# A two-layer hybrid encoder in fp32: another order of VectorE's work around the attention, and the gating of seven convolution rows on GpSimd

## The reference, cut to what matters

```
proj = h @ w_in                       # q, k, v, z, x/B/C, dt: 1024 -> 3872 columns
q, k = rope(q), rope(k)               # 8 query heads, 2 key heads of 64
attn = window_attention(q, k, v)      # |i-j| <= 128, blocks of 128 queries, a sink logit per head
xbc  = silu(conv5(xbc) + b)           # depthwise, width 5, centred; 12 rows of 128 channels
y    = ssd forward + ssd backward + D * x     # Mamba-2, chunks of 128
ssd  = rms_norm(y * silu(z)) * g
h    = layer_norm(alpha * h + [attn, ssd] @ w_out)
gate, val = h @ w_up                  # 2 x 2816
h    = layer_norm(alpha * h + (silu(conv3(gate)) * val) @ w_down)
```

## Time and profile before

| | before |
|---|---|
| median of 3 runs | 1300.85 us |
| the profiled execution | 1301.02 us, its span 1299.2 us |
| TensorE busy | 1280.8 us (99% of the span) |
| VectorE busy | 798.3 us (61%) |
| ScalarE busy | 611.7 us (47%) |
| GpSimd busy | 125.4 us (10%) |
| TensorE's granted clock | 0.999 of full speed |

### The profile page before, as it was taken

One profiled execution on the slowest core, in us unless ns is written; L12 is line 12 of the kernel. 1 busy time (PEld: TensorE's weight loads), 2 busy tenths in 40 slices (PEclk: granted clock), 3 DMA queues, 4 the chain that ended last, 5 costly groups with the idle time before them and its releaser, 6 DMA issues.

```text
span 1299.2 us, 17967 instructions
## 1 busy us (share of the span) xinstructions
PE 1280.8 (99%) x7456; PEld 1059.1 (82%) x7456; DVE 798.3 (61%) x1071; ACT 611.7 (47%) x913; POOL 125.4 (10%) x125
## 2 busy tenths in 40 slices
PE   9999999999999999999999999999999999999997
PEld 9877778889888888888898677778888888888886
DVE  7888898865444444342378988979654444443425
ACT  6767776436333333311286776653553333332112
POOL 2024611001000000000020344000100000000000
PEclk9999999999999999999999999999999999999999
DMA  5464666523323333323144557663233333323322
GB/s 199 158 145 111 134 146 134 176 76 103 98 98 98 97 97 98 130 97 98 53 136 143 132 115 163 130 179 122 73 113 96 97 95 96 96 95 128 97 96 110
DMA packets 43872, 151.36 MB, mean 116 GB/s; under 512 B 4912, under 2 KB 9424, under 8 KB 42640
## 3 DMA queue, kind: packets, MB, share of 16 engines
q1 hardware_dynamic: 38160, 130.01, 30.3%
q0 software_dynamic: 5632, 20.21, 9.3%
HBM read 141.81 MB, written 6.29 MB: 114 GB/s over the span
## 4 chain that ended last, share of the span: by engine, by line
PE 93%; DVE 5%; ACT 1%; issue 1%; DMA 0%; POOL 0%; SPq 0%; DVEq 0%
PE ps L869 18%; PE ps L870 17%; PE ps L871 17%; PE ps L1027 9%; PE ps L1028 9%; PE ps L1029 9%; PE ps L916 5%; PE ps L1241 2%; DVE cv L1476 2%; PE ps L895 1%; PE ps L1255 1%; PE ps L1019 1%; PE ps L1225 1%; DVE ast L1624 1%; DMA raw<-in_units 0%
## 5 line engine op out<-in xcount | busy, mean ns | idle before, releaser
L869 PE MATMUL ps<-hhi,whi 128*128 128x512 f32 x1040 | 410.4, 395 | 4.4 <-DVE cv L1476 3.0
L870 PE MATMUL ps<-hlo,whi 128*128 128x512 f32 x1040 | 405.1, 389 | 0.0
L871 PE MATMUL ps<-hhi,wlo 128*128 128x512 f32 x1040 | 405.0, 389 | 0.0
L618 ACT ACTIVATE whi<-raw 128x1024 fp32r<-128x1024 f32 x208 | 219.5, 1057 | 216.1 <-DMA raw<-in_units 216.1
L1313 DVE TENSOR_TENSOR wlo<-raw,whi 128x1024 fp32r<-128x1024 f32 x170 | 207.9, 1225 | 149.6 <-ACT whi L618 149.6
L869 PEld LDWEIGHTS ps<-hhi,whi 128*128 128x128 f32 x1040 | 195.1, 188 | 53.3 <-issue 7.9
L871 PEld LDWEIGHTS ps<-hhi,wlo 128*128 128x128 f32 x1040 | 195.2, 188 | 41.2
L870 PEld LDWEIGHTS ps<-hlo,whi 128*128 128x128 f32 x1040 | 195.3, 188 | 39.1
L1027 PE MATMUL ps<-whi,uhi 128*128 128x512 f32 x352 | 137.1, 390 | 0.0
L1029 PE MATMUL ps<-wlo,uhi 128*128 128x512 f32 x352 | 137.0, 389 | 0.0
L1028 PE MATMUL ps<-whi,ulo 128*128 128x512 f32 x352 | 136.9, 389 | 0.0
(11 more groups left out here) (182 smaller groups left out, 1540.8 us busy)
## 6 DMA issues: line engine op xcount, KB each, us to landing
raw<-in_units SPq DMA_DIRECT2D x208, 512.0 KB, 3.6
wlo<-in_units POOLq DMA_DIRECT2D x38, 512.0 KB, 5.5
gb<-in_gb SPq DMA_DIRECT2D x5, 1024.0 KB, 5.7
h_kept<-hb SPq DMA_DIRECT2D x2, 2048.0 KB, 9.0
ha<-h_kept SPq DMA_DIRECT2D x2, 2048.0 KB, 9.7
hb<-in_x SPq DMA_DIRECT2D x4, 512.0 KB, 5.9
v_rep<-v_tm SPq DMA_DIRECT2D x32, 64.0 KB, 2.2
out_y<-hb SPq DMA_DIRECT2D x8, 256.0 KB, 2.0
```

The costliest lines, as they stand in the source:

```text
L618: A(whi[:, m % RING, :], raw[:, m % RING, :], ACT.Copy).then_inc(unit_hi, 1)
L869: mm(out, whi[:, slot, cols], xhi, start=start, stop=False)
L870: mm(out, whi[:, slot, cols], xlo, start=False, stop=False)
L871: return mm(out, wlo[:, slot, cols], xhi, start=False, stop=stop)
```

## The change

The schedule and four engines' code for these entries change; the arithmetic is the same.

1. `A0` goes from 8 to 7: each attention turn is one step earlier. `AV_AT` now puts the values products into projections 11, 13, 15 and 16 (before: 11, 13, 15 and 17): relative to the turns they need, blocks 0 to 2 are one projection later, block 3 as before.
2. In an attention step VectorE's order was: mask and maximum, transpose of the last turn, gating of the last row, weight splitting, the first tap or two, denominator, the other taps. It is now: mask and maximum, three taps, denominator, last tap, transpose of the last turn. The taps are four entries (F, F1, F2, F3).
3. The gating of rows 1 to 7 (`SILU_POOL`) is a multiplication on GpSimd, ahead of XS and AN in its step. ScalarE adds the 1 by a second instruction after the tanh (a Copy with bias 1.0), which waits for the tanh. Rows 0 and 8 to 11 stay with VectorE.
4. Unit 11's low part is made by DMA too (`BY_DMA` from 11), so no attention step has a splitting on VectorE.
5. The first scores wait for 3 rotated rows (k and two of q) and the second for all 5, as needed.

```diff
-BY_DMA = range(12, 31)
+BY_DMA = range(11, 31)
+SILU_POOL = range(1, 8)
-A0 = 8
-AV_AT = {A0 + 2 * t + 3: t for t in range(NBLK)}
+A0 = 7
+AV_AT = {A0 + 4: 0, A0 + 6: 1, A0 + 8: 2, A0 + 9: 3}
@@ mixer_schedule
-        if 1 <= i < 9:
-            steps += [("PT", i - 1), ("SIL2", n - 1 - U_CONV)]
-            if n - 1 - U_CONV >= 4:
-                steps += [("XS", n - 1 - U_CONV)]
+        if n - 1 - U_CONV in SILU_POOL:
+            steps += [("SIL2", n - 1 - U_CONV)]
+        if i == 8:
+            steps += [("PT", 7)]
...
         steps += [("SH" if n >= U_CONV else "S", n + AHEAD)]
+        if 1 <= i <= 8 and n - 1 - U_CONV >= 4:
+            steps += [("XS", n - 1 - U_CONV)]
         steps += [("F", n)]
...
-        if 2 <= i < 8:
-            steps += [("F1", n)]
+        if U_CONV <= n < U_Z:
+            steps += [("F1", n), ("F2", n)]
         if 0 <= i < 8:
             steps += [("AD", i), ("AN", i)]
-        if U_CONV <= n < U_Z and not 2 <= i < 8:
-            steps += [("F1", n)]
         if U_CONV <= n < U_Z:
-            steps += [("F2", n)]
+            steps += [("F3", n)]
+        if i == 1:
+            steps += [("SIL2", n - 1 - U_CONV)]
+        if 1 <= i < 8:
+            steps += [("PT", i - 1)]
@@ gpsimd
+                    elif what == "SIL2" and i in SILU_POOL:
+                        pool.wait_ge(conv_tanh, L * N_CONV + i + 1)
+                        pool.wait_ge(silu_done, L * N_CONV + i)
+                        x = bc[:, i, :] if i < 4 else xsc[:, i % 2, :]
+                        nc.gpsimd.tensor_tensor(x, x, cv[:, i % 2, :], ALU.mult).then_inc(silu_done, 1)
@@ scalar
-                        A(dst, cv[:, i % 2, :], ACT.Tanh, scale=0.5).then_inc(conv_tanh, 1)
+                        if i in SILU_POOL:
+                            A(dst, cv[:, i % 2, :], ACT.Tanh, scale=0.5).then_inc(tanh_raw, 1)
+                            act.wait_ge(tanh_raw, L * len(SILU_POOL) + i - SILU_POOL[0] + 1)
+                            A(dst, dst, ACT.Copy, bias=1.0).then_inc(conv_tanh, 1)
+                        else:
+                            A(dst, cv[:, i % 2, :], ACT.Tanh, scale=0.5).then_inc(conv_tanh, 1)
@@ tensor
-                        if i == 0:
-                            pe.wait_ge(rope_done, L * 5 + 5)
-                        else:
+                        if i < 2:
+                            pe.wait_ge(rope_done, L * 5 + (5 if i else 3))
+                        if i:
                             pe.wait_ge(as_exp, L * 8 + i)
@@ vector
-                    elif what == "SIL2":
+                    elif what == "SIL2" and i not in SILU_POOL:
                         dve.wait_ge(conv_tanh, L * N_CONV + i + 1)
+                        if i - 1 in SILU_POOL:
+                            dve.wait_ge(silu_done, L * N_CONV + i)
```

More of the change, by code:

```diff
@@ L335, in trunk @@
         v_done, tanh_done, zs_done = sem("v_done"), sem("tanh_done"), sem("zs_done")
-        v_spread = sem("v_spread")
+        v_spread, tanh_raw = sem("v_spread"), sem("tanh_raw")
         xd_done, seg_full = sem("xd_done"), sem("seg_full")
@@ L1464, in _ @@
                         split(unit(L, i))
-                    elif what in ("F", "F1", "F2") and U_CONV <= i < U_Z:
+                    elif what in ("F", "F1", "F2", "F3") and U_CONV <= i < U_Z:
                         j = i - U_CONV
@@ L1470, in _ @@
                         src = ps[:, unit_bank(i), :].rearrange("p (b s) -> p b s", b=NSEQ)
[L1471 to L1478, removed]
-                    elif what == "SIL2":
+                        n, tap = {"F": (0, 0), "F1": (1, 1), "F2": (2, 3), "F3": (3, 4)}[what]
+                        s = tap - 2
+                        lo, hi = max(0, -s), SEQ - max(0, s)
+                        if n:
+                            dve.wait_ge(conv_taps, L * 4 * N_CONV + 4 * j + n)
+                        V.scalar_tensor_tensor(out=dst[:, :, lo:hi], in0=src[:, :, lo + s:hi + s],
+                                               scalar=pmc("conv_w", 5 * j + tap, 5 * j + tap + 1),
+                                               in1=dst[:, :, lo:hi], op0=ALU.mult, op1=ALU.add).then_inc(conv_taps, 1)
+                    elif what == "SIL2" and i not in SILU_POOL:
                         dve.wait_ge(conv_tanh, L * N_CONV + i + 1)
+                        if i - 1 in SILU_POOL:
+                            dve.wait_ge(silu_done, L * N_CONV + i)
                         x = bc[:, i, :] if i < 4 else xsc[:, i % 2, :]
```

## The result

| | before | after |
|---|---|---|
| median | 1300.76 us (1300.68 to 1300.94, 4 runs) | 1308.81 us (1306.22 to 1310.91, 4 runs) |
| ratio, 95% interval | | 1.006 (1.0048 to 1.0072) |
| profiled execution, its span | 1301.02, 1299.2 | 1310.91, 1309.1 |
| TensorE, VectorE, ScalarE, GpSimd busy | 1280.8, 798.3, 611.7, 125.4 | 1285.1, 793.9, 619.0, 145.8 |
| TensorE's granted clock | 0.999 | 0.995 |

In e5 and e6 one run of ten took several times as long as the others; it is left out of the ranges given for them, and without it their medians are 0.04 and 0.11 us lower than printed.

The account below looks back on a forecast made before the run. TensorE was taken to wait for VectorE's round (7.42 against 6.73 us) and, at SF 0, a chain off TensorE. Both layers together gain 2.5 or lose 0.3 us: 1298.4 to 1301.2, middle 1299.7; range 1295.2 to 1302.6.

Parts of the forecast that it names:

- The gap at SF 0: TensorE before SF 0, end of the chain: a wait of 2.0 us stays, and behind SF 0 nothing is changed.
- the 14.88 from T 7: Chain from T 7 to SF 0: gating ready 4.75 us after T 7, SF 0 another 10.13 later.
- Block 3 in unit 16: Values block 3 on TensorE: moves its 2.3 us ahead of T 7.
- the small operations held: VectorE's 4-column operations, if held by GpSimd: waits up to T 7 of 3.3 us, SF 0 at 153.55.
- row 0's gating: VectorE, step 8: arrives 0.4 us inside GpSimd's scaling, is held until 77.10, ends at 77.66 instead of 76.15.
- AS 3: Scores on TensorE due at 81.98: wait 1.44 us because mask 2 and its exponentials come late.
- rival (a): Step 8: GpSimd holds nothing up, row 0's gating gets in first or between the scaling's instructions; 1295.4 us, chance 0.24.
- the 3.05 row: Step 17 before the change: VectorE's gating of row 10 took 3.05 us instead of 0.65, held through two GpSimd instructions.
- CB 1: TensorE's product needing `alo` of block 1: waits about 0.2 us, or 0.62 if the small operations are held.
- The small terms: Across engines: Copy 0.63 us, GpSimd's gating 1.3, the values' transpose wait gone, 10.13 from gating 9 to SF 0.
- Rival (c): GpSimd's gating starts up to 0.9 us later, meeting small operations in full: 2.2 us more per layer, 1305.6 us, chance 0.15.
- the held case: Whole kernel if VectorE's 4-column operations are held by GpSimd: 0.2 us lost per layer, 1301.2 us as timed.

Follow-up runs that it names:

- e5: The kernel after with GpSimd's product with D (XS) behind its scaling in attention steps: 1303.72 us, ratio 1.0018; no usable trace.
- e6: The kernel after with the gating of rows 1 to 7 back on VectorE, ahead of the taps, and no Copy on ScalarE: 1301.18 us, ratio 0.9999.
- e10: The kernel before with two further caps of 1.14 us each on VectorE, so SF 0 comes 2.28 us later per layer: 1308.74 us, ratio 1.0062.
- e4: The kernel after with values block 3 back in unit 17: 1300.16 us, ratio 0.9993.
- e7: The kernel after with row 10's XS before heads 2 and 3, attention steps' XS behind the scaling, and values block 3 in unit 17: 1294.74 us, ratio 0.9953.
- e1: The kernel after with XS of row 10 ahead of heads 2 and 3 on GpSimd in step 17: 1301.71 us, ratio 1.0005.
- e11: The same edit as e5 on the kernel after (XS behind the scaling in attention steps), run again: 1303.49 us, ratio 1.0015.
- e8: The kernel after once more, unchanged: 1308.33 us, ratio 1.0061.
- e2: The kernel before with XS of row 10 ahead of heads 2 and 3 on GpSimd in step 17: 1298.50 us, ratio 0.9981.
- e3: The kernel before with one more 1.14 us cap on VectorE ahead of the cap that SF 0 waits for: 1304.69 us.
- e9: The kernel after with rows 1 to 7 gated on VectorE, row 10's XS before heads 2 and 3, and values block 3 in unit 17: 1293.05 us, ratio 0.9939.

## Why the prediction was wrong, step by step

- **The gap at SF 0: right in size, wrong in price.** "So a wait of 2.0 us stays at SF 0" and "behind SF 0 nothing is changed". The wait was 2.08 and 2.10. Priced at its own length it is all in the 14.88 from T 7; but behind it TensorE ran 3.4 us at half clock, 1.6 us more, once per layer. This is the step that failed: the kernel before had 0.71 and 1.48 us there, and I counted 2.0 us as more of the same. e10 shows the price on the kernel before, without any of the change.
- **Block 3 in unit 16: the second step that failed.** I moved its "2.3 us ahead of T 7" and looked no further. In layer 1 it cost 3.71 us of stop and 1.7 of half clock. e4 shows that the place does it. The stop of 1.34 us behind block 3 in the trace of before was a sign that I left unread. What stops TensorE is open (below).
- **Up to SF 0 in layer 0 the sum was right, its parts not.** T 7 was forecast for 138.7 with the small operations held; it came at 139.16, or 138.4 without the 0.74 of the start, and SF 0 at 153.56 on that clock against 153.55. That the two agree so closely is luck: T 7 was 0.25 early, and from there SF 0 took 15.14 us, not 14.88. And of the parts, row 0's gating was held for 0.46 us, not 1.5: it got in between the scaling's two instructions, whose pair took 2.49 instead of 2.04 us, so AS 3 waited 0.26 and not 1.44. Here rival (a) was right, and with it my reading of the 3.05 row, held over such a gap, was too strong: in step 17 it held again (2.90), in step 8 not. Against that CB 1 waited 2.11 instead of 0.62 us.
- **CB 1: a term that I took from the wrong end.** I let XS start when the DMA issue's 0.9 us were over; the next instruction starts 0.59 us after the issue's start (103.54 to 104.13). So XS reached L1644 of turn 5, and that is 1.5 us. Whether 4 columns are held was left open in the prediction: they are, 0.33, 0.76 and 1.67 us instead of 0.16.
- **The small terms.** The Copy took 0.63, GpSimd's gating 1.27 to 1.30, the values had no wait ahead of them, gating 9 to SF 0 took 10.12: all as forecast.
- **Rival (c)**, slower by late GpSimd work, named 1305.6 and the right meetings, but not what made it dear. It priced the held operations at 2.2 us per layer; they cost 1.5 per layer more than forecast, at CB 1, and the rest of the loss is clock and stop. Of e7's 14 us against the kernel after, e1's edit alone gave 7 and e4's over 8; they overlap, since each takes the wait at SF 0.
- **The range.** Its upper end was the sum of waits. Each of three long gaps had a further price that no term had, 4.9 us in the profiled execution, and the stop 3.7: with the 1301.2 of the held case and the start's 0.74 that gives 1310.5, against 1310.9.

## What to carry to other kernels

Where TensorE is busy for 99% of the time, look at the longest single wait of it and not only at their sum: here the four waits of 0.64 us before the values cost 2.6 us, and one wait of 2.1 us cost 2.1 or 3.7. A change that gathers waits into one can be dear even where the sum stays, and one that breaks a long one up, as the swap of two entries in step 17 does, gives more than its length. Before work goes to an idle engine, list what each instruction of it will run beside: a 4-column operation that stands in the way of ScalarE made 1.3 us of GpSimd's spare time cost 1.5 us of TensorE's. And when a kernel's runs scatter by several us where another's agree within 0.3, read the granted clock by stretches before explaining the median.

## What the runs showed of the hardware that I had not expected

- *TensorE's clock.* After idle time of 2.07 to 2.63 us the granted clock fell to 0.50 in 8 of 18 cases, after 2.97 to 3.77 in 4 of 5, after 1.48 and 1.79 in neither. It stays there for up to 3.4 us, with TensorE fully busy, and costs 1.4 to 1.7 us. The length of the gap does not settle it: e6 and e11 each had two gaps of 2.08 us at SF 0, and the clock fell at the second alone; at CB 1 it fell in e4 (2.09 and 2.08 us) and not in the kernel after (2.11 and 2.14). The Trainium skill (TensorE: Matmul & The Clock Gate, section Part 1: The HAM clock gate) says of the rise to the upper clock at a kernel's start that it is run-variable, since the chip's watch on activity runs free of the kernel. The runs agree in so far as the fall, too, comes at one gap and not at another of the same length; what decides it no run here shows. Why CB 1 is hit less often than SF 0 (2 of 8, 6 of 10) is open.
- *The stop.* With block 3 in unit 16, layer 1 stops after exactly 98 of 128 matmuls in each of the five profiles with block 3 there (the kernel after, e1, e6, e8, e11), for 3.71, 3.71, 0.97, 3.16 and 1.79 us; TensorE's weight loads stop with it. The place is fixed and the length is not. Stops of over 0.8 us that no engine is named for stand in other kernels too: right behind block 3 of layer 0 in the kernel before, e2, e3 and e10 (1.34, 1.31, 1.06, 1.34 us), before its 128th matmul in e7 (0.86), and in unit 15 of layer 1, behind block 2, in e7, e8 and e11 (0.84, 0.84, 1.04). The queue for instructions has 59 packets of 16 KB in the whole span, and in the even stretches of the kernel after (324 to 620 us) one starts every 116 to 134 matmuls. In 12 of these 13 stops TensorE goes on 2.2 to 2.5 us after such a packet starts (the 13th, e7's 0.86: 3.05). In the kernel after the packet starts at 780.18, 1.50 us into the stop; in e6, where the stop was 0.97, it starts 1.41 ahead of it. So the stop is long where the packet starts late. That TensorE waited for its instructions fits all this, but it was only argued: no run changed the number of instructions ahead of the place, and why the packet starts late is open. With block 3 in unit 17 no profile has a stop within block 3 of layer 1 (e4, e7, e9 and the four of the kernel before and its variants).
- *GpSimd's DMA issue* is shown as 0.87 us long, but the next GpSimd instruction starts 0.59 to 0.61 us after it began (103.54 to 104.13, 147.80 to 148.41).
